# Expert rows through DRAM tables by slot, stationary router weights and tiles at multiples of 512 bytes in a two-layer decoder kernel

## The chip, the cores and the metric

The kernel runs on one core of one Trainium2 chip. The metric is the device time of one execution in microseconds (us), here 1588.71 us as the median of 3 runs (1586.83 to 1590.33). One execution was recorded by the hardware profiler. The engines are named as in the profile: PE is TensorE's matrix multiplier (PEld its weight loads), DVE is VectorE, ACT is ScalarE, POOL is GpSimd and SP is SyncE. SP and POOL issue DMA transfers.

## The reference

The trunk has two layers over 256 tokens of width 1024, in float32. Each layer does a mixer (a combined projection, sparse attention and a pooling branch, merged and projected back) and then a channel mixer. In layer 0 the channel mixer is a dense SwiGLU, in layer 1 it is a mixture of 8 experts of which each token uses the best two. The change touches the second one:

```python
def moe_swiglu(h, w_router, w1, w3, w2):
    logits = jnp.einsum('bsd,de->bse', h, w_router)
    top_v, top_i = lax.top_k(logits, 2)
    top_w = jax.nn.softmax(top_v, axis=-1)
    gate = jnp.sum(one_hot(top_i, 8) * top_w[..., None], axis=-2)
    y = jnp.zeros_like(h)
    for e in range(8):
        y = y + gate[..., e:e + 1] * ((silu(h @ w1[e]) * (h @ w3[e])) @ w2[e])
    return y          # w1, w3: 8 x 1024 x 3584, w2: 8 x 3584 x 1024
```

## The kernel before

**Precision and weights.** Every large product is made of three matmuls in a reduced-precision float32 form: an operand is split into a high and a low part, and high by high, high by low and low by high are added in PSUM (`three`, lines 744 to 748). Weights come in chunks of 128 x 2048 or 128 x 1024 floats. SP loads a chunk into `w_raw`, ACT rounds it to `w_hi` (line 448 in layer 1's experts, 442 elsewhere), DVE subtracts to get `w_lo` (line 1125 or 1120), and PE multiplies. `w_hi` and `w_lo` have four slots each. The raw chunks have four slots in the layers and eight in the expert stage, where `w_raw` holds chunks with number modulo 8 below 4 and `w_raw_456` and `w_raw_7` the others. Both splits wait for PE to free a slot, so they run up to four chunks ahead of it. SP loads up to eight chunks ahead. Each engine's instructions are written out in order by hand, and semaphores join them. There is no scheduler.

**Expert jobs.** Tokens are sorted to experts in jobs of up to 128 rows. The number of jobs is read from a table and is 8 on these inputs (112 SiLU instructions of 14 blocks each). A job has 28 up chunks (w1 and w3 side by side, 14 blocks of 2 chunks, 12 matmuls of 512 columns per chunk) and 28 down chunks (6 matmuls each). After each block ACT takes the SiLU (line 695), DVE multiplies (line 1536), PE transposes the product (line 1060), and ACT and DVE split it again (lines 700 and 1542).

**Rows in and out.** DVE writes for each job a selection matrix `select` with a one where token and slot meet (`select`, line 1461). PE gathers the job's rows already transposed by 32 matmuls of 128 columns, x high and low against `select` (`gather`, line 1034), and ACT and DVE scale and split them (lines 680 and 1515). The gather of job i+1 stands between the up and the down part of job i. For the way back PE transposes `select` (line 1078), and after the down part ACT and DVE split the result y in two (lines 737 and 1577). PE scatters it to token order by 8 matmuls of 512 columns (`scatter`, line 1045). This is placed in the next job, after the first chunk of its second block. DVE then adds the rows times the gate to `x_residual` (line 1523). Job 0 scatters zeros, which POOL has written (line 423). After the last job the scatter comes once more, and SP stores the output (line 408).

**Routing.** Before the jobs PE multiplies h by the router weights with h as the stationary operand, 48 matmuls of 8 columns. DVE takes the norm's inverse root, the logits (line 1430), the two best experts and a mask. PE counts positions with five small fp32 matmuls (lines 1020 to 1024), DVE writes the low part of the token rows (line 1448), the selection for job 0 and the job table.

## Time and profile before

| | |
|---|---|
| profiled execution, device time | 1589.16 us |
| its span, first to last instruction | 1587.3 us |
| PE busy | 1547.0 us, 97% of the span |
| DVE busy | 1267.5 us, 80% |
| ACT busy | 1052.3 us, 66% |
| DMA, mean over the span | 281 GB/s, 445.32 MB |
| DMA from 40 to 200 us, in layer 0 | 129 to 186 GB/s |
| mean granted TensorE clock | 0.988 of full speed |

A busy share is an average. PE is pipelined, so a PE that is always busy can still issue at less than its best rate, and the starts of matmuls tell more than their durations. In the expert stage a matmul of 512 columns lasts 0.39 us in the records, while the next one starts 0.23 us after it. The clock is given as a share of full speed, 1.00 for 2.4 GHz and 0.50 for 1.2 GHz. A releaser in square brackets is what ended an engine's idle time.

### The profile page before, as it was taken

The numbers are of one execution on the slowest core, as the hardware profiler recorded it, in microseconds if no ns is written. First come the engines' busy times: TensorE is split into PE (matmuls) and PEld (weight loads), VectorE is DVE, ScalarE is ACT, GpSimd is POOL, SyncE is SP. The second block draws the span as 40 slices with busy tenths as digits, with TensorE's granted clock in tenths as the row PEclk, the third lists the DMA queues.
The fourth block names the chain that finished last, engine by engine and source line by source line (L and its number), as shares of the span: only waits on it lengthen the run. The fifth ranks groups of instructions, "written<-read, shape, count | busy, mean of one in ns | idle before, by whom it ended". The sixth has DMA issues, their size and how long they took to land.

```text
span 1587.3 us, 22532 instructions
## 1 busy us (share of the span) xinstructions
PE 1547.0 (97%) x7253; PEld 1270.7 (80%) x7253; DVE 1267.5 (80%) x1329; ACT 1052.3 (66%) x1159; POOL 5.9 (0%) x12
## 2 busy tenths in 40 slices
PE   7999999999999899999999999999999999999997
PEld 6888888788888778878878878877887887887885
DVE  5885655446976579799789789799889979978978
ACT  6565544336464467687687687687778768768766
POOL 0000000000000000000000000000000000000000
PEclk9999999999999789999999999999999999999998
DMA  9543565358543669799899999999989989989985
GB/s 333 160 162 129 186 202 167 106 190 283 167 160 108 234 228 305 262 367 371 290 379 370 313 362 367 330 340 371 373 299 372 373 292 367 369 296 376 372 296 195
DMA packets 329116, 445.32 MB, mean 281 GB/s; under 512 B 14144, under 2 KB 269160, under 8 KB 329080
## 3 DMA queue, kind: packets, MB, share of 16 engines
q1 hardware_dynamic: 328512, 442.71, 81.8%
q0 software_dynamic: 480, 2.13, 0.4%
q8 instruction: 20, 0.33, 0.1%
q14 instruction: 16, 0.13, 0.0%
q10 hardware_dynamic: 88, 0.02, 0.0%
HBM read 443.76 MB, written 1.05 MB: 280 GB/s over the span
## 4 chain that ended last, share of the span: by engine, by line
PE 83%; DMA 4%; issue 4%; DVE 4%; ACT 3%; SPq 1%; DVEq 0%; ACTq 0%
PE bank L746 26%; PE bank L748 25%; PE bank L747 25%; DMA w_raw<-in_moe_w 4%; PE bank L1034 2%; ACT w_hi L448 2%; PE bank L1060 2%; DVE w_lo L1125 1%; DVE hT_lo L1515 1%; SPq L351 1%; PE bank L828 1%; DMA w_raw<-in_w_in 1%; PE bank L772 1%; ACT hT_hi L737 0%; PE bank L812 0%
## 5 line engine op out<-in xcount | busy, mean ns | idle before, releaser
L1125 DVE TENSOR_TENSOR w_lo<-w_raw,w_hi 128x1024 fp32r<-128x1024 f32 (+1 forms) x448 | 780.7, 1755 | 110.8 <-ACT w_hi L448 110.2
L448 ACT ACTIVATE w_hi<-w_raw 128x1024 fp32r<-128x1024 f32 (+1 forms) x448 | 663.8, 1492 | 157.6 <-PE bank L748 143.8
L746 PE MATMUL bank<-w_hi,hT_hi 128*128 128x512 f32 (+1 forms) x1424 | 567.5, 399 | 6.6 <-DVE hT_lo L1515 2.5
L748 PE MATMUL bank<-w_hi,hT_lo 128*128 128x512 f32 (+1 forms) x1424 | 554.9, 390 | 0.0
L747 PE MATMUL bank<-w_lo,hT_hi 128*128 128x512 f32 (+1 forms) x1424 | 553.6, 389 | 0.0
L746 PEld LDWEIGHTS bank<-w_hi,hT_hi 128*128 128x128 f32 x1424 | 268.7, 189 | 62.3 <-issue 6.8
L748 PEld LDWEIGHTS bank<-w_hi,hT_lo 128*128 128x128 f32 x1424 | 268.5, 189 | 56.6
L747 PEld LDWEIGHTS bank<-w_lo,hT_hi 128*128 128x128 f32 x1424 | 269.2, 189 | 50.8
L1120 DVE TENSOR_TENSOR w_lo<-w_raw,w_hi 128x2048 fp32r<-128x2048 f32 (+2 forms) x100 | 201.5, 2019 | 95.6 <-ACT w_hi L442 94.8
L442 ACT ACTIVATE w_hi<-w_raw 128x2048 fp32r<-128x2048 f32 (+2 forms) x100 | 169.6, 1699 | 160.1 <-PE bank L748 158.6
L746 PE MATMUL bank<-w_hi,hiddenM_hi 128*128 128x512 f32 x448 | 178.7, 399 | 1.1
L748 PE MATMUL bank<-w_hi,hiddenM_lo 128*128 128x512 f32 x448 | 176.8, 395 | 0.0
L747 PE MATMUL bank<-w_lo,hiddenM_hi 128*128 128x512 f32 x448 | 176.7, 394 | 0.0
L695 ACT ACTIVATE hiddenM<-bank 128x256 f32<-128x256 f32 x112 | 42.8, 382 | 99.2 <-PE bank L748 99.2
L746 PEld LDWEIGHTS bank<-w_hi,hiddenM_hi 128*128 128x128 f32 x448 | 84.4, 188 | 23.3 <-DVE w_lo L1125 4.6
L748 PEld LDWEIGHTS bank<-w_hi,hiddenM_lo 128*128 128x128 f32 x448 | 84.4, 188 | 19.7
L747 PEld LDWEIGHTS bank<-w_lo,hiddenM_hi 128*128 128x128 f32 x448 | 84.5, 189 | 18.7
L1536 DVE TENSOR_TENSOR hiddenM<-hiddenM,bank 128x256 f32<-128x256 f32 x112 | 46.0, 410 | 7.9 <-ACT hiddenM L695 6.9
L1060 PE MATMUL bank<-shape_constants,hiddenM 128*128 128x128 f32 x224 | 43.1, 274 | 7.0 <-DVE hiddenM L1536 7.0
L1060 PEld LDWEIGHTS bank<-shape_constants,hiddenM 128*128 128x128 f32 x224 | 29.5, 139 | 25.0 <-DVE hiddenM L1536 13.8
L1542 DVE TENSOR_TENSOR hiddenM_lo<-bank,hiddenM_hi 128x256 fp32r<-128x256 f32 x112 | 46.6, 416 | 0.0
L700 ACT ACTIVATE hiddenM_hi<-bank 128x256 f32 (+1 forms) x112 | 41.2, 368 | 0.2 <-PE bank L1060 0.2
(230 smaller groups left out, 1022.9 us busy)
## 6 DMA issues: line engine op xcount, KB each, us to landing
w_raw<-in_moe_w SPq DMA_DIRECT2D x672, 512.0 KB
w_raw<-in_w_in SPq DMA_DIRECT2D x64, 512.0 KB
w_raw<-in_dense_w SPq DMA_DIRECT2D x44, 512.0 KB
w_raw<-in_dense_w SPq DMA_DIRECT2D x44, 256.0 KB
w_raw<-in_w_out SPq DMA_DIRECT2D x16, 512.0 KB
w_raw<-in_w_pool_proj SPq DMA_DIRECT2D x8, 512.0 KB
w_raw<-in_w_attn_proj SPq DMA_DIRECT2D x8, 512.0 KB
w_raw<-in_w_in SPq DMA_DIRECT2D x8, 296.0 KB
```

Of the source, the lines that this page charges most:

```text
L442: act.activation(whi[:, c % SLOTS, 0:n], raw[:, c % SLOTS, 0:n], ACT.Copy).then_inc(s_hi, 1)
L448: act.activation(whi[:, m % SLOTS, 0:n], raw8[m % 8][:, 0:n], ACT.Copy).then_inc(s_hi, 1)
L695: act.activation(hsM[:, q, :], bank[4 + q][:, 0:256], ACT.Silu).then_inc(m_si, 1)
L700: act.activation(dst, bank[q][:, 0:256].rearrange("p (k t) -> p k t", t=P), ACT.Copy).then_inc(m_fhi, 1)
L746: pe.matmul(dst, ahi, bhi, start=start, stop=False)
L747: pe.matmul(dst, ahi, blo, start=False, stop=False)
L748: return pe.matmul(dst, alo, bhi, start=False, stop=stop)
L1060: ins = pe.transpose(bank[q][:, f * P:f * P + P], hsM[:, q, f * P:f * P + P], ident)
L1120: dve.tensor_tensor(wlo[:, s, 0:n], raw[:, s, 0:n], whi[:, s, 0:n], ALU.subtract).then_inc(s_lo, 1)
L1125: dve.tensor_tensor(wlo[:, m % SLOTS, 0:n], raw8[m % 8][:, 0:n], whi[:, m % SLOTS, 0:n], ALU.subtract).then_inc(s_lo, 1)
L1536: dve.tensor_tensor(hsM[:, q, :], hsM[:, q, :], bank[4 + q][:, 256:512], ALU.mult).then_inc(m_hm, 1)
L1542: dve.tensor_tensor(lo, bank[q][:, 0:256].rearrange("p (k t) -> p k t", t=P), hi, ALU.subtract).then_inc(m_flo, 1)
```

## The change

**Rows by slot.** The kernel gets two tables in DRAM, `x_by_slot` and `y_by_slot`, with 12 x 128 rows of 1024 floats. During layer 0 SP copies parts of x into all of the first and a part of the second, 16 transfers of 512 KB. After routing, ACT scales the token rows once more into `x_scaled_rows`, and POOL writes them to their slots by four indirect transfers of 512 KB (128 rows of 4 KB), one for each half of the tokens and each of their two choices. Each later job loads its 128 rows with one SP transfer, and PE only transposes them (8 fp32 transposes). Job 0 is still gathered by `select`. After a job's down part ACT copies y to SBUF in fp32, and SP stores it to `y_by_slot`. The scatter, its selection transposes, y's low part and DVE's additions in the loop are gone. After the last job POOL gathers each token's two rows by four indirect transfers, and DVE adds them with their gates.

**Router.** The router weights are now the stationary operand: 24 matmuls with 8 output rows and 256 columns. PE transposes the 8 x 256 result back. DVE's norm moves behind the copy of that result. ACT loads its square root table earlier. DVE writes the low part of the second half of the rows after the selection instead of before. `keep_busy` adds 22 matmuls of 512 columns, whose results nobody reads, at four places.

**Addresses.** The small tensors are allocated first, with a pad of 48 words, so that the large ones start at multiples of 512 bytes. Before, in each partition, `w_raw` started at 128 modulo 512 bytes, and `w_raw_7` and `w_raw_456` at 256 modulo 512.

```diff
+        sq0 = sb("sqrt_first", [P, 16])
+        sb("align_512", [P, 48])
+        raw = sb("w_raw", [P, SLOTS, FULL])
+        whi = sb("w_hi", [P, SLOTS, FULL], FR)
+        wlo = sb("w_lo", [P, SLOTS, FULL], FR)
+        X = sb("x_residual", [P, TT, D])
+        hThi = sb("hT_hi", [P, KC, S], FR)
+        hTlo = sb("hT_lo", [P, KC, S], FR)
         ident = cst[:, C_ID:C_ID + P]
 
...
         moe.close()
+        late = ExitStack()
+        sb("late_raws", [P, 4, FULL], F32, late)
+        xg = sb("x_slot_rows", [P, D], F32, late)
+        ysb = sb("y_slot_rows", [P, D], F32, late)
+        y0 = sb("y_first_choice", [P, TT, D], F32, late)
+        sb("late_hidden", [P, D], F32, late)
+        xn = sb("x_scaled_rows", [P, TT, D], F32, late)
+        yg = [[y[:, t, :] for t in range(TT)] for y in (y0, xn)]
+        late.close()
+        xslot = nc.dram_tensor("x_by_slot", (NJ * P, D), F32).ap()
+        yslot = nc.dram_tensor("y_by_slot", (NJ * P, D), F32).ap()
...
-                for col in ZCOL:
+                fill = [xslot[P * j:P * j + P, :] for j in range(NJ)] + [yslot[P * j:P * j + P, :] for j in range(E, NJ)]
+                for q, col in enumerate(ZCOL):
                     for h in range(2):
                         load(c, k_halves(c, w, 512 * h, col, 512))
+                        if l == 0:
+                            if c == 2:
+                                sp.wait_ge(s_x, 16)
+                            sp.dma_start(fill[2 * q + h], X[:, h, :]).then_inc(s_xz, 16)
                         c += 1
...
                 group(up_chunk, i, e, 24, 6)
+                sp.wait_ge(s_xsc, 2 * TT * 16)
+                sp.wait_ge(s_g, i * 2 + 2)
+                sp.dma_start(xg[:], xslot[bass.ds(i * P + P, P), :]).then_inc(s_xg, 16)
                 group(down_chunk, i, e, 28, 0)
                 with sp.Fori(0, 3) as it:
                     for u in range(2):
                         group(down_chunk, i, e, 32 + 4 * u, it * 2 + (1 + u), it * 8)
 
+            def store_y(i):
+
+                sp.wait_ge(m_y, i * 2 + (LEAD + 2))
+                sp.dma_start(yslot[bass.ds(i * P, P), :], ysb[:]).then_inc(s_ys, 16)
+
             def next_job(i, e):
 
                 for g in range(2):
                     group(up_chunk, i, e, JOB_CHUNKS + 4 * g, g)
+                store_y(i)
...
+            store_y(njobs - 1)
+            sp.wait_ge(s_ys, njobs * 16 + 16)
+            sp.nop().then_inc(s_go, 1)
             for t in range(TT):
-                sp.wait_ge(m_xa, njobs * 4 + (2 * t + 2))
+                sp.wait_ge(m_xa, 2 * t + 2)
                 sp.dma_start(out[0, t * P:t * P + P, :], X[:, t, :]).then_inc(s_out, 16)
...
-            pool.wait_ge(s_rt, 1)
-            for z in (yhi, ylo, selT[:]):
-                ins = pool.memset(z.bitcast(F32), 0.0)
-            ins.then_inc(s_y0, 1)
+            pool.wait_ge(s_xz, (2 * NJ - E) * 16)
+            pool.wait_ge(s_row, 1)
+            for c in range(2):
+                for t in range(TT):
+                    if c == 0:
+                        pool.wait_ge(s_xn, t + 1)
+                    pool.indirect_dma_start(xslot, bass.IndirectOffsetOnAxis(rowu[:, c * TT + t:c * TT + t + 1], 0),
+                                            xn[:, t, :], None).then_inc(s_xsc, 16)
+            pool.wait_ge(s_go, 1)
+            for t in range(TT):
+                for c in range(2):
+                    pool.indirect_dma_start(yg[c][t], None, yslot,
+                                            bass.IndirectOffsetOnAxis(rowu[:, c * TT + t:c * TT + t + 1], 0)
+                                            ).then_inc(s_yg[c * TT + t], 16)
...
+                else:
+                    act.activation(sq0[:, 0:1], cst[:, C_ONE:C_ONE + 1], ACT.Sqrt)
...
             gathered_hi(0)
+            for t in range(TT):
+                act.activation(xn[:, t, :], X[:, t, :], ACT.Copy, scale=st[:, 3, t:t + 1]).then_inc(s_xn, 1)
+            act.nop().then_inc(m_y, LEAD)
+            act.nop().then_inc(s_ys, 16)
...
@@ -709,8 +757,7 @@
                         if not (first and u == 0):
                             hid_hi_m(b - 1, 1 - u)
                         if first and u == 1:
-                            act.wait_ge(s_st, i + 1)
-                            act.activation(selT[:], bank[1][:, 0:S], ACT.Copy).then_inc(s_sts, 1)
+                            act.wait_ge(s_xsc, 2 * TT * 16)
                         silu_m(b, u)
...
                 act.wait_ge(s_use, i * JOB_CHUNKS + (MOE0 + JOB_CHUNKS))
+                act.wait_ge(s_ys, i * 16 + 16)
                 for j in range(2):
-                    act.activation(yhi[:, 4 * j:4 * j + 4, :], bank[6 + j][:].rearrange("p (k n) -> p k n", n=P),
-                                   ACT.Copy).then_inc(m_yhi, 1)
+                    act.activation(ysb[:, 512 * j:512 * j + 512], bank[6 + j][:], ACT.Copy).then_inc(m_y, 1)
                 split_m(d0 + 27, FULL, j8)
...
+            def keep_busy(n, b):
+
+                for _ in range(n):
+                    pe.matmul(bank[b][:], aThi[:, 0, 0:P], aThi[:, 0:2, :], start=True, stop=True)
+
             layer(1, LAYER1, first=lambda: x_T(2, 1))
+            keep_busy(4, 5)
             x_T(3, 1)
...
                 for k in (2 * j, 2 * j + 1):
-                    for t in range(TT):
-                        ins = three(bank[4 + t][:, 0:E], hThi[:, k, t * P:t * P + P], hTlo[:, k, t * P:t * P + P],
-                                    wrhi[:, k, :], wrlo[:, k, :], k == 0, k == KC - 1)
+                    ins = three(bank[4][0:E, 0:S], wrhi[:, k, :], wrlo[:, k, :], hThi[:, k, :], hTlo[:, k, :],
+                                k == 0, k == KC - 1)
             ins.then_inc(s_rt, 1)
+            pe.wait_ge(s_lt, 1)
+            for t in range(TT):
+                ins = pe.transpose(bank[5][:, t * E:t * E + E], lgT[:, t * P:t * P + P], cst[0:E, C_ID:C_ID + E])
+            ins.then_inc(s_rl, 1)
+            keep_busy(9, 0)
...
+            keep_busy(3, 0)
 
             def gather(i):
 
-                pe.wait_ge(s_sel, i + 1)
+                if isinstance(i, int):
+                    pe.wait_ge(s_sel, 1)
+                    for t in range(TT):
+                        pe.wait_ge(s_xrl, t + 1)
+                        for j in range(2):
+                            for q in range(4):
+                                k = 4 * j + q
+                                for x in (xrhi, xrlo):
+                                    ins = pe.matmul(bank[2 + j][:, q * P:q * P + P], x[:, t, k * P:k * P + P],
+                                                    selR[:, t, :], start=(t == 0 and q == 0 and x is xrhi),
+                                                    stop=(t == TT - 1 and x is xrlo), skip_group_check=True)
+                            if t == TT - 1:
+                                ins.then_inc(s_g, 1)
+                    return
+                pe.wait_ge(s_xg, i * 16)
                 for j in range(2):
                     for q in range(4):
                         k = 4 * j + q
-                        for t in range(TT):
-                            for x in (xrhi, xrlo):
-                                ins = pe.matmul(bank[2 + j][:, q * P:q * P + P], x[:, t, k * P:k * P + P],
-                                                selR[:, t, :], start=(t == 0 and x is xrhi),
-                                                stop=(t == TT - 1 and x is xrlo))
+                        ins = pe.transpose(bank[2 + j][:, q * P:q * P + P], xg[:, k * P:k * P + P], ident)
                     ins.then_inc(s_g, 1)
...
-            pe.wait_ge(s_xrl, 2)
             gather(0)
-            pe.wait_ge(s_y0, 1)
+            keep_busy(6, 0)
             pe.wait_ge(s_tab, 1)
...
                         chunk(c, [bank[4 + u][:]], hehi, helo, 0, 512, True, False, i * jd + it, tiles=1)
-                        if first and u == 1:
-                            scatter(i)
                         if not (first and u == 0):
                             if not first:
                                 pe.wait_ge(m_flo, i * NB_E + b - 2 + LEAD)
                             hiddenT_m(b - 1, 1 - u)
-                        if first and u == 1:
-                            for t in range(TT):
-                                ins = pe.matmul(bank[1][:, t * P:t * P + P], selR[:, t, :], identR[:],
-                                                start=True, stop=True)
-                            ins.then_inc(s_st, 1)
...
-                pe.wait_ge(m_xa, i * 4 + 4)
                 gather(i + 1)
...
-                        pe.wait_ge(m_xa, i * 4 + 4)
+                        pe.wait_ge(m_y, i * 2 + LEAD)
...
-            scatter(njobs)
...
             dve.wait_ge(s_rt, 1)
+            dve.tensor_copy(lgT, bank[4][0:E, 0:S]).then_inc(s_lt, 1)
+            norm(3)
+            dve.wait_ge(s_rl, 1)
             for t in range(TT):
-                ins = dve.tensor_scalar(lg[:, t, :], bank[4 + t][:, 0:E], st[:, 3, t:t + 1], None, ALU.mult)
+                ins = dve.tensor_scalar(lg[:, t, :], bank[5][:, t * E:t * E + E], st[:, 3, t:t + 1], None, ALU.mult)
...
+            rows_lo(0)
             dve.wait_ge(s_pos, 1)
...
+            for t in range(TT):
+                ins = dve.tensor_scalar(selR[:, t, :], cst[:, C_IOTA:C_IOTA + P], pm[:, t, 0:1], None, ALU.is_equal)
+            ins.then_inc(s_sel, 1)
+            rows_lo(1)
...
+            iotas = cst[:, C_IOTA:C_IOTA + E].rearrange("p (o e) -> p o e", o=1)
+            dve.tensor_tensor(picke[:], pick[:], iotas.broadcast_to([P, nq, E]), ALU.mult)
+            dve.tensor_scalar(past[:], pm[:], float(P), None, ALU.is_ge)
+            dve.scalar_tensor_tensor(rowe[:], iotas.broadcast_to([P, TT, E]), float(P), pm[:], ALU.mult, ALU.add)
+            chain(dve.scalar_tensor_tensor(one8, iota8, -1.0, rank, ALU.mult, ALU.add))
+            dve.tensor_reduce(tabf[:, E:NJ], picke[:], AX.X, ALU.add)
+            chain(dve.tensor_scalar(one8, one8, float(E - 2), float(P), ALU.add, ALU.mult))
+            chain(dve.tensor_tensor(past[:], past[:], ov[:, 3:4, :].broadcast_to([P, TT, E]), ALU.mult))
             dve.tensor_copy(tabi[:], tabf[:]).then_inc(s_tab, 1)
-            chain(dve.tensor_scalar(posj[:, :, E:NJ].rearrange("p t q -> p q t"), pickr[:], -float(P), None, ALU.add))
+            chain(dve.tensor_tensor(rowe[:], rowe[:], past[:], ALU.add))
+            for c, m in enumerate((m0, m1)):
+                ins = dve.tensor_tensor(rowc[:, c], m[:], rowe[:], ALU.mult)
+            chain(ins)
+            chain(dve.tensor_reduce(rowf[:], rowc[:].rearrange("p c t e -> p (c t) e"), AX.X, ALU.add))
+            dve.tensor_copy(rowu[:], rowf[:]).then_inc(s_row, 1)
 
...
-                        if 1 <= b <= 4:
-                            add_rows(i, (b - 1) // 2, (b - 1) % 2)
-                        if b == 5:
-                            dve.wait_ge(s_st, i + 1)
-                            select(i + 1)
...
-                for j in range(2):
-                    dve.wait_ge(m_yhi, i * 2 + j + 1)
-                    dve.tensor_tensor(ylo[:, 4 * j:4 * j + 4, :], bank[6 + j][:].rearrange("p (k n) -> p k n", n=P),
-                                      yhi[:, 4 * j:4 * j + 4, :], ALU.subtract).then_inc(m_ylo, 1)
                 split_m(d0 + 27, FULL, j8)
             for t in range(TT):
-                for nh in range(2):
-                    add_rows(njobs, t, nh)
+                for c in range(2):
+                    dve.wait_ge(s_yg[c * TT + t], 16)
+                    if c:
+                        dve.wait_ge(m_xa, 2 * t + 1)
+                    dve.scalar_tensor_tensor(X[:, t, :], yg[c][t], pr[:, 2 + c, t:t + 1], X[:, t, :],
+                                             ALU.mult, ALU.add).then_inc(m_xa, 1)
...
```

On PE, in the second block of each job, before: `select` is the selection matrix, `hT_hi` and `hT_lo` in line 1045 hold y's parts, and `hiddenM` is the block's product.

```order
L748 MATMUL bank<-w_hi,hT_lo 128x512
L1045 MATMUL bank<-hT_hi,selectT 128x512
L1045 MATMUL bank<-hT_lo,selectT 128x512
...
L1058 REGISTER_ALU
L1060 MATMUL bank<-shape_constants,hiddenM 128x128 x2
L1078 MATMUL bank<-identity_r,select 128x128 x2
L756 REGISTER_ALU
L746 MATMUL bank<-w_hi,hT_hi 128x512
```

And at the same place now:

```order
L795 MATMUL bank<-w_hi,hT_lo 128x512
L1115 REGISTER_ALU
L1117 MATMUL bank<-shape_constants,hiddenM 128x128 x2
L803 REGISTER_ALU
L793 MATMUL bank<-w_hi,hT_hi 128x512
```

The eight scatter matmuls and the two of the selection are gone, so the transposes of the product follow the first chunk directly. At the gather of the next job PE now has, where 32 matmuls of line 1034 stood:

```order
L1135 COMPARE_AND_BRANCH
L1100 ISA
L1104 MATMUL bank<-shape_constants,x_slot_rows 128x128 x8
L1143 REGISTER_ALU
L1147 ISA
L793 MATMUL bank<-w_hi,hiddenM_hi 128x512
```

Only the 8 transposes of the loaded rows are left between up and down part. On SP the load of these rows stands between the last up chunk and the first down chunk of a job, and in another place the store of y behind the second group of the next job's up chunks:

```order
L372 DMA w_raw<-in_moe_w 128x4x256 x2
L393 ISA
L394 ISA
L394 DMA x_slot_rows<-x_by_slot 128x1024
L383 REGISTER_ALU
L377 ISA
L377 DMA w_raw<-in_moe_w 128x1024
...
L402 REGISTER_ALU
L403 ISA
L403 DMA y_by_slot<-y_slot_rows 128x1024
```

Both wait on SP for a semaphore (the gather before, and y in SBUF), and the chunk loads behind them wait with them.

## Rows read from the trace of the kernel before

**Rows 1.** The page's chain that ended last: shares of the span by engine.
```profile
PE 83%; DMA 4%; issue 4%; DVE 4%; ACT 3%; SPq 1%; DVEq 0%; ACTq 0%
```

**Rows 2.** Windows from gather to gather: length, each engine's busy us, clock, DMA share, GB/s.
```profile
770.88:897.12 126.24, 125.39 (x576) 102.06 (x575) 112.29 (x100) 95.04 (x97) 0.00 (x0) 1.00 1.01 349
...
sum 886.34, PE 877.26 PEld 714.46 DVE 786.51 ACT 665.37 POOL 0.00; mean PE 125.32 PEld 102.07 DVE 112.36 ACT 95.05 POOL 0.00
```

**Rows 3.** Timeline of TensorE, one steady gather: start, duration, engine, line, operation.
```profile
770.88 0.23 PE L1034 MATMUL bank<-select,x_rows_hi 128*128 128x128 f32 x1
...
774.41 0.45 PE L746 MATMUL bank<-w_hi,hiddenM_hi 128*128 128x512 f32 x1
```

**Rows 4.** Timeline of TensorE in layer 1: eight fp32 transposes between matmuls.
```profile
529.13 0.39 PE L748 MATMUL bank<-w_hi,hT_lo 128*128 128x512 f32 x1
529.36 1.04 PE L772 MATMUL bank<-shape_constants,x_residual 128*128 128x128 f32 x8
...
530.47 0.39 PE L747 MATMUL bank<-w_lo,hT_hi 128*128 128x512 f32 x1
```

**Rows 5.** Timeline of all engines, end of one expert job and start of the next.
```profile
814.45 1.92 ACT L448 ACTIVATE w_hi<-w_raw 128x2048 fp32r<-128x2048 f32 x1 [0.56 <-DMA w_raw<-in_moe_w]
...
822.77 0.40 PE L1045 MATMUL bank<-hT_hi,selectT 128*128 128x512 f32 x1
...
824.88 0.41 DVE L1536 TENSOR_TENSOR hiddenM<-hiddenM,bank 128x256 f32<-128x256 f32 x1
...
825.35 0.44 PE L1060 MATMUL bank<-shape_constants,hiddenM 128*128 128x128 f32 x2 [0.55 <-DVE hiddenM L1536]
```

**Rows 6.** DMA throughput in 40 slices of 3.25 us, from 700 to 830 us.
```profile
GB/s 381 350 348 354 385 385 385 382 348 349 355 384 386 385 381 348 349 367 422 418 387 266 171 161 134 271 260 284 338 413 417 413 368 348 349 352 385 386 385 379
```

**Rows 7.** Waits over the span: engine, line, what for, total us, times, longest.
```profile
ACT w_hi L448 <- DMA w_raw<-in_moe_w: 13.6, 17, 1.1
```

**Rows 8.** Timeline of TensorE, first job, where the empty scatter stands.
```profile
570.51 0.41 PE L1045 MATMUL bank<-hT_hi,selectT 128*128 128x512 f32 x1
...
572.37 0.38 PE L1060 MATMUL bank<-shape_constants,hiddenM 128*128 128x128 f32 x2
```

**Rows 9.** Windows in the routing stage and at the first job's start.
```profile
537.50:550.00 12.50, 8.62 (x41) 8.44 (x40) 6.95 (x28) 7.02 (x10) 2.12 (x3) 0.50 1.08 377
...
560.00:565.00 5.00, 5.00 (x12) 3.98 (x13) 3.68 (x12) 1.66 (x3) 0.00 (x0) 0.52 0.29 97
```

**Rows 10.** Timeline of the routing stage, all engines.
```profile
538.87 1.28 ACT L474 ACT_TABLE_LOAD   x1
...
541.20 0.16 DVE L1151 TENSOR_TENSOR norm_stats<-norm_stats 128x2 f32<-128x2 f32 x1
...
543.86 0.36 DVE L1430 TENSOR_SCALAR router_logits<-bank,norm_stats 128x8 f32<-128x8 f32 x2 [2.51 <-PE bank L748]
...
546.78 2.48 DVE L1448 SCALAR_TENSOR_TENSOR x_rows_lo<-x_residual,norm_stats,x_rows_hi 128x1024 fp32r<-128x1024 f32 x2
...
557.07 0.41 PE L1034 MATMUL bank<-select,x_rows_lo 128*128 128x128 f32 x1
...
559.97 0.79 PE L746 MATMUL bank<-w_hi,hT_hi 128*128 128x512 f32 x1 [2.48 <-DVE hT_lo L1515]
```

**Rows 11.** Timeline of the end of the kernel.
```profile
1574.99 1.06 ACT L737 ACTIVATE hT_hi<-bank 128x512 fp32r<-128x512 f32 x2
...
1581.53 2.71 DVE L1523 SCALAR_TENSOR_TENSOR x_residual<-bank,gate_by_job,x_residual 128x512 f32<-128x512 f32 x4
...
1582.95 1.65 SPq L408 DMA_DIRECT2D out<-x_residual  x2
```

**Rows 12.** DMA issues: queue, count, KB each, median us from issue to landing.
```profile
x_residual<-in_x SPq DMA_DIRECT2D x1, 1024.0 KB, 6.7
out<-x_residual SPq DMA_DIRECT2D x2, 512.0 KB, 2.7
...
w_router<-in_moe_router POOLq DMA_DIRECT2D x1, 32.0 KB, 8.4
```

86 lines of the change are left out of this document (23 added, 63 removed).

## The prediction

> **What bounds the kernel now.** I read the chain that ended last first. PE is 83% of it and DMA 4% [rows 1], so what counts is how fast PE issues. Next came windows cut from one gather to the next, since the expert jobs are most of the span. Seven of them take 886.34 us, 126.62 us a job, all at full clock, with PE busy 125.3 us, DVE 112.4 us and ACT 95.0 us of it, and DMA at 349 GB/s [rows 2]. PE paces the job and the DMA is close behind. What one removed instruction is worth is therefore read from starts on PE's timeline, and only where PE doesn't then wait for something else [rows 3 to 5]. Then the DMA's rate inside a job [rows 6, 7], the routing stage [rows 9, 10] and the end [rows 11, 12].
>
> **Gathers.** From the first of 32 matmuls to the next matmul it is 774.41 - 770.88 = 3.53 us [rows 3]. Eight fp32 transposes between matmuls of 512 columns stretch 529.13 to 530.47 us. Less two matmul starts of 0.23 us, that is 0.88 us [rows 4]. The gathers for jobs 1 to 8 each save 2.65 us (the last one's rows go unused, but it runs): 21.2 us. The load of the slot rows is queued before the first down chunk, some twelve chunks ahead of PE, and is hidden by them. If it were late, PE would stop for up to 2.7 us, a 512 KB transfer [rows 12].
>
> **Scatter and selection transposes.** The eight scatter matmuls start at 822.77 us and the block's transposes at 825.35 us, with 0.55 us of idle PE in between. PE waits there for DVE's product, which ends at 824.88 + 0.41 = 825.29 us [rows 5]. This product stays where it is when the scatter goes, because it ends a chain on ACT and DVE: a split, the copies of y, a split, the SiLU table, a split, SiLU, a split, the product. So the 1.86 us of the scatter turn into waiting. The chain begins with 0.56 us of waiting for DMA at 814.45 us [rows 5]. I count those 0.56 us as won at seven job starts, 3.9 us, because the DMA gets faster (below). The bounds are 0, and 7 x 1.1 us, the longest such wait [rows 7]: 7.7 us. In job 0 nothing is waited for, and the scatter's 572.37 - 570.51 = 1.86 us go in full [rows 8]. Two selection matmuls at 3.53/32 = 0.11 us each, in eight jobs: 1.8 us. DVE loses its additions (4 x 0.68 us from [rows 11]) and y's low part. It had room, so this is worth nothing by itself.
>
> **Routing.** Before, the logits start at 543.86 us because the router's matmuls end late. The norm ends at 541.20 + 0.16 us, and 1.28 us of that chain was a table load [rows 10]. Now 24 matmuls replace 48, and the norm ends the path, 1.28 us earlier for the table and about 0.6 us later for the copy of the 8 x 256 logits that it follows: 540.8 us, 3.1 us won. The selection follows one row split of 2.48/2 = 1.24 us instead of two, and one small copy fewer: 1.4 us. The gather takes 557.07 - 550.42 + 0.21 = 6.86 us, because the clock was granted at 0.50 here [rows 9, 10]. With the added matmuls in the pauses I take it at full clock, 3.5 us: 3.3 us won. DVE's longer table of rows now stands ahead of the low parts that PE waits for: about 0.7 us lost. Together the first job starts 7.1 us earlier than 559.97 us. Its first 12 matmuls took 5.0 us at clock 0.52 [rows 9]. At 0.23 us each it is 2.8 us: 2.2 us won. The 22 added matmuls (5 us in all) lie in pauses of 1.4 to 2.9 us. If the clock stays at 1.2 GHz they fill them exactly.
>
> **Start.** SP now waits for x, which lands 6.7 us after its issue [rows 12], and puts a 512 KB transfer before chunk 3. At 385 GB/s [rows 6] that is 1.36 us on a chunk that PE needs several us later. I take 0.5 us between 0 and 1.4. The 16 fills are 22 us of DMA time spread beside layer 0's first block products, where the queue moves less than half of what rows 6 show possible. POOL's four writes to the slots start at about 552 us, and at 2.7 us each end at 563 us. ACT waits for them before the second block's SiLU at about 564 us, so they are just covered.
>
> **End.** y is copied at 1574.99 + 1.06 = 1576.05 us, and the kernel ends at 1587.3 us [rows 11]. Now follow the store (0.3 us to issue, 2.7 us), four indirect gathers, one addition of 1.24 us and the output transfer of 2.8 us. No row shows an indirect transfer. The four lie between 2.7 + 3 x 1.36 = 6.8 us (overlapping at 385 GB/s) and 4 x 8.4 us, the POOL transfer at the crowded start [rows 12]. I take 4 x 2.7 = 10.8 us, by the row for transfers of this size. The end is then 1593.9 us: 6.6 us lost, between 2.6 and 29.4. The Trainium skill (DMA: Bandwidth & Descriptors, "Anatomy of one DMA — SWDGE (gpsimd) path") gives about 2 us plus bytes at 436 GB/s for a transfer from POOL. By that one is 3.2 us, four in a row 12.8 us, and the end 2 us later. No row shows it.
>
> **Addresses.** Within the up part the DMA runs at 381 to 386 GB/s in some slices and 348 to 355 in others, in turns of about four [rows 6]. Four chunks take about as long as such a turn, and the slow turn is the last one before the down chunks, which start in `w_raw_456`: the slow slots are those of `w_raw`, at 128 modulo 512 bytes, the fast ones lie at 256. So I take all up chunks at 385 GB/s. A job's DMA is then 29.4 MB/385 + 14.7 MB/418 + 1.05 MB/385 = 76.3 + 35.1 + 2.7 = 114 us (before: 80 + 35), under PE's new 126.62 - 2.65 - 0.22 - 0.56 = 123.2 us. Store and load of rows then fit. The Trainium skill (same page, "How a descriptor splits into AXI transactions") says that a run that doesn't start at 256 bytes pays for an extra partial transaction; the trace agrees as far as 348 against 385 can.
>
> **Sum.** Won: 21.2 + 3.9 + 1.9 + 1.8 + 7.1 + 2.2 = 38.1 us. Lost: 6.6 + 0.5 = 7.1 us. Net 31.0 us from the profiled execution's 1589.16 us (span 1587.3 us): 1558.2 us. That execution was 0.4 us above the median, so 1558 us.
>
> **Rivals.** *The clock falls in routing all the same* (18%). The large pause for the mask remains, nearly 2 us after the nine fillers. Then the gather's 3.3 us and the 2.2 us aren't won: 1563 or 1564 us. *The waits for DMA stay*, because addresses aren't the reason for the two rates (8%): the 3.9 us go, 1562 us. *The DMA paces the jobs* (4%): this is the slower side. If 349 GB/s [rows 2] is all it can give over a job, 44.04 + 1.05 MB take 129.2 us, 2.6 us more than now. The seven jobs lose 18 us instead of gaining 24, and with the rest the time is about 1601 us. It decides once a job's DMA passes 123.2 us, at 366 GB/s. Against it stand 385 and 418 GB/s for tens of us, and slices of 134 to 171 in the down part where nothing is left to load [rows 6]. *A ceiling just above* (3%): the Trainium skill (same page, "Where 436 GB/s comes from") has the HBM side bind at about 358 GB/s. As a mechanism it is the same one. The 45.09 MB would take 126.0 us, the loop would stay as it is, and only routing and end would change: 1580 us. The slices above 380 speak against it. *POOL's indirect transfers are slow* (4%), 8.4 us each in a row: the slots are written at 586 us, PE stops some 20 us, and the end costs 29.4 us: 1602 us. Even with 6.9 us each they would eat the whole gain. *It doesn't do what it says* (1%): row slots beside the path, no change.
>
> **How the numbers follow.** My case has 62%: 1558 us. With its own bounds (job starts 0 to 7.7, end 2.6 upwards, start 0 to 1.4) it spans 1551 to 1564. The clock and DMA-wait rivals end inside 1564. Up to 1567 for both together, the range 1550 to 1567 leaves out the 12% of the other cases and a few per cent of mine. A measurement of this kernel can tell about 0.2%, 3 us, from no change. Slower by more: 4 + 4%, less a little where a slow POOL is only half as slow: 6%. Same: 2%. Faster: 92%.
>
> **What would show it.** Right: steady jobs of 123.2 us from gather to gather; the transposes in 0.9 us; at the second block a PE wait of about 2 us for DVE's product where the scatter was; no ACT waits for `w_raw` there; up slices all near 385 GB/s; the first expert matmul near 553 us into the span at clock 1.00; 18 us from y's copy to the end. Wrong: jobs above 125 us, a DMA share at its top all through the down part, PE waiting for the slot rows or ACT for the slot writes, or an end of over 25 us.

## The result and the profile after

The changed kernel takes 1560.33 us (median of 4 runs, 1559.3 to 1560.9), the kernel before 1589.32 us on the same chip: a ratio of 0.9818, 95% interval 0.9803 to 0.9832. The forecast was 1558 us, between 1550 and 1567. The profiled execution has a span of 1558.9 us against 1587.3 us before, so 28.4 us are to be accounted for, where the sum of the prediction had 31.0.

Cut at the same four places as before, the span reads like this (us, from TensorE's timeline):

| stretch | before | after | won | forecast |
|---|---|---|---|---|
| start to the first expert matmul | 559.97 | 554.16 | 5.8 | 6.6 |
| from there to the first steady gather (job 0) | 83.97 | 82.07 | 1.9 | 4.3 |
| seven jobs, gather to gather | 886.34 | 861.96 | 24.4 | 24.0 |
| last gather to the end | 57.02 | 60.71 | -3.7 | -3.9 |

The windows from gather to gather, after: length, then busy us of TensorE, its weight loads, VectorE, ScalarE and GpSimd, the granted clock, DMA's share and GB/s. They answer to [rows 2].
```profile
636.23:760.35 124.12, 121.26 (x542) 98.80 (x541) 109.05 (x92) 94.65 (x96) 0.00 (x0) 0.99 1.02 364
760.35:882.63 122.28, 119.90 (x541) 97.54 (x540) 108.80 (x92) 94.67 (x96) 0.00 (x0) 1.00 1.02 370
882.63:1007.07 124.44, 121.28 (x542) 98.76 (x541) 109.17 (x92) 94.79 (x96) 0.00 (x0) 0.99 1.01 362
...
sum 861.96, PE 842.02 PEld 685.28 DVE 762.58 ACT 662.86 POOL 0.00; mean PE 120.29 PEld 97.90 DVE 108.94 ACT 94.69 POOL 0.00
```
A job takes 123.14 us instead of 126.62, as forecast (123.2). But TensorE is busy for 120.3 us of it, where before it was busy for 125.3 of 126.6: there are now 2.8 us of waiting in a job instead of 1.3. And two of the seven jobs are about 1.6 us longer than the rest, with a clock below 1.00.

TensorE at one steady gather, after (answers to [rows 3]): start, duration, what.
```profile
882.39 0.40 PE L795 MATMUL bank<-w_hi,hT_lo 128*128 128x512 f32 x1
882.63 1.03 PE L1104 MATMUL bank<-shape_constants,x_slot_rows 128*128 128x128 f32 x8
883.42 0.48 PE L793 MATMUL bank<-w_hi,hiddenM_hi 128*128 128x512 f32 x1
```
It is 883.42 - 882.63 = 0.79 us to the next matmul, where it was 3.53. No wait stands ahead of it: the slot rows are there.

TensorE in the down part, 18 matmul starts apart, first before, then after:
```profile
789.74 0.39 PE L746 MATMUL bank<-w_hi,hiddenM_hi 128*128 128x512 f32 x1
...
793.93 0.39 PE L746 MATMUL bank<-w_hi,hiddenM_hi 128*128 128x512 f32 x1
```
```profile
889.89 0.40 PE L793 MATMUL bank<-w_hi,hiddenM_hi 128*128 128x512 f32 x1
...
893.99 0.39 PE L793 MATMUL bank<-w_hi,hiddenM_hi 128*128 128x512 f32 x1
```
The starts are (793.93 - 789.74)/18 = 0.233 us apart before and (893.99 - 889.89)/18 = 0.228 after; over all jobs the means are 0.2327 and 0.2272. The whole down part takes 38.78 us instead of 39.50.

ScalarE, VectorE and TensorE at the end of one job and the start of the next, after (answers to [rows 5]); a bracket is the idle time just before and what ended it.
```profile
804.70 1.28 ACT L739 ACT_TABLE_LOAD   x1
...
806.11 1.90 ACT L491 ACTIVATE w_hi<-w_raw 128x2048 fp32r<-128x2048 f32 x1
...
808.04 2.29 DVE L1173 TENSOR_TENSOR w_lo<-w_raw,w_hi 128x2048 fp32r<-128x2048 f32 x1 [0.94 <-ACT w_hi L491]
...
810.25 0.41 DVE L1573 TENSOR_TENSOR hiddenM<-hiddenM,bank 128x256 f32<-128x256 f32 x1
...
810.72 0.44 PE L1117 MATMUL bank<-shape_constants,hiddenM 128*128 128x128 f32 x2 [1.71 <-DVE hiddenM L1573]
```
Where the scatter stood, TensorE waits 1.71 us for VectorE's product (1.7 to 2.65 us in the seven jobs), as forecast. From the last down matmul to these transposes it is 11.32 us as the mean of the seven jobs, where it was 11.88: 0.56 us less, also as forecast.

DMA throughput from 700 to 830 us, 3.25 us a slice (answers to [rows 6]), and the waits for it over the span.
```profile
GB/s 387 384 386 385 384 387 384 386 385 385 386 384 386 401 420 421 357 281 199 199 260 333 197 324 369 396 416 412 381 384 385 385 385 386 401 382 386 385 385 386
```
```profile
ACT w_hi L491 <- DMA w_raw<-in_moe_w: 21.2, 28, 1.5
...
ACT hiddenM L743 <- DMA x_by_slot<-x_scaled_rows,row_of_choice: 3.3, 1, 3.3
```
All slices of the up part are at 385 now; those at 348 are gone. Yet ScalarE waits longer for weights in all (21.2 us against 13.6 in [rows 7]). A new wait of 3.3 us, in job 0, is for GpSimd's writes to the slots.

The end, after (answers to [rows 11]).
```profile
1539.52 1.06 ACT L785 ACTIVATE y_slot_rows<-bank 128x512 f32<-128x512 f32 x2
...
1540.76 0.35 SPq L403 DMA_DIRECT2D y_by_slot<-y_slot_rows  x1
1543.71 2.09 POOL L465 DMA_INDIRECT y_first_choice<-y_by_slot,row_of_choice  x1 [980.79 <-SPq L438]
...
1549.13 1.28 DVE L1613 SCALAR_TENSOR_TENSOR x_residual<-y_first_choice,gate_probs,x_residual 128x1024 f32<-128x1024 f32 x1 [4.19 <-DMA y_first_choice<-y_by_slot,row_of_choice]
...
1552.61 3.69 SPq L441 DMA_DIRECT2D out<-x_residual  x2
...
1554.65 1.28 DVE L1613 SCALAR_TENSOR_TENSOR x_residual<-x_scaled_rows,gate_probs,x_residual 128x1024 f32<-128x1024 f32 x1
```
From y's copy (ends 1540.58) to the end at 1558.9 it is 18.3 us (forecast: 18). The store takes 2.95 us, the first indirect read 5.4 us to its addition, and the four overlap.

One more view, the page's chain that ended last, now reads "issue 63%; PE 33%" instead of "PE 83%" [rows 1], though TensorE is busy for 97% of the span before and 96% after. It is no measure of what changed.

### The profile page after: what moved, and what is told of

It reads as the page before. It is cut to its first block, busy times and chain, and to the rows that moved or that the text cites. A ratio compares the mean times of both kernels' runs of the same rounds, so it can differ in the third digit from the quotient of the medians.

```text
span 1558.9 us, 21888 instructions
## 1 busy us (share of the span) xinstructions
PE 1501.7 (96%) x6973; PEld 1230.8 (79%) x6973; DVE 1241.6 (80%) x1264; ACT 1051.4 (67%) x1153; POOL 16.1 (1%) x17
## 4 chain that ended last, share of the span: by engine, by line
issue 63%; PE 33%; DVE 1%; DMA 1%; POOL 1%; ACT 0%; POOLq 0%; SPq 0%; ACTq 0%; DVEq 0%
PE bank L793 10%; PE bank L795 10%; PE bank L794 10%; PE bank L875 1%; DMA w_raw<-in_w_in 1%; PE bank L819 1%; POOL x_by_slot L460 0%; PE bank L1094 0%; PE bank L859 0%; DMA y_first_choice<-y_by_slot,row_of_choice 0%; PE bank L930 0%; PE bank L1007 0%; PE bank L910 0%; PE bank L847 0%; PE bank L938 0%
```

## The experiments

Each ran in three rounds beside the kernel before. Times are medians of 4 runs; those of the kernel before in the same sessions were 1589.3 to 1590.0 us. Where three numbers stand in brackets, they are the ratio to the kernel before and its 95% interval. "The job" is the mean of the seven windows of one profiled execution.

Small differences need care. (6), (7), (8) and (10) come out 1.6 to 3.5 us below the changed kernel, and the interval of each overlaps the changed kernel's (0.9803 to 0.9832). What they show is therefore read stage by stage in the profiled executions. How much these vary by themselves can be seen in (5), (7), (9), (10) and (11), whose edits lie outside TensorE's work in the seven jobs: 859.95 to 862.88 us for the seven.

| kernel | time, us | job, us | down part, us |
|---|---|---|---|
| before | 1589.3 | 126.62 | 39.50 |
| before, all at 512 (1) | 1577.3 | 125.15 | 38.79 |
| changed, addresses of before (2) | 1579.3 | 125.01 | 39.55 |
| changed, w_raw at 128 (3) | 1572.7 | 124.88 | 38.78 |
| changed, all off (4) | 1598.4 | 128.20 | 39.05 |
| changed | 1560.3 | 123.14 | 38.78 |
| changed, four more edits (12) | 1548.9 | 121.71 | 38.78 |

**1. The addresses alone, in the kernel before.**
```
+        sb("align_512", [P, 64])
         raw = sb("w_raw", [P, SLOTS, FULL])     # and the other large tiles, behind the small ones
```


> The kernel before with one change: the small tensors stand first and a pad follows, so that every large tile starts at a multiple of 512 bytes. Theory: the addresses alone make two things that the trace after shows: the up part's loads all run at about 385 GB/s (before in turns 348 and 385), and the down part, whose matmuls started 0.2327 us apart, gets 0.2272 us and 38.8 us a job instead of 39.5. With about 0.5 us less waiting at each job's start that is 8 x 0.72 + 7 x 0.5 = 9 us: about 1580 us, seven jobs of 125.4 us instead of 126.6. Rival: the down part got faster because DVE's additions and y's low part are gone; then only the DMA's slices change, the down part stays at 39.5 us, and the time is 1585 to 1589 us.


Measured: 1577.34 us (0.993, 0.9913 to 0.9948). The down part takes 38.79 us, with all the DVE work still in it, and the boundary is 0.76 us shorter (11.12 us from the last down matmul to the second block's transposes, against 11.88). The windows:
```profile
768.46:893.51 125.05, 124.47 (x575) 102.06 (x574) 112.19 (x100) 94.95 (x97) 0.00 (x0) 1.00 0.99 353
...
sum 876.06, PE 871.16 PEld 714.22 DVE 785.75 ACT 664.73 POOL 0.00; mean PE 124.45 PEld 102.03 DVE 112.25 ACT 94.96 POOL 0.00
```
The theory holds, and it gave more than expected: 10.3 us in the seven jobs. The addresses are a gain of their own, on TensorE as well. The up part's slices are all at about 385 GB/s.

**2. The changed kernel at the addresses of before** (w_raw, w_hi, w_lo at 128 modulo 512 bytes, w_raw_7 and w_raw_456 at 256).
```
-        sb("align_512", [P, 48])                # large tiles first again
+        sb("sqrt_pad", [P, 112])
```


> The changed kernel with all large tiles at the addresses that they have in the kernel before (w_raw, w_hi and w_lo at 128 modulo 512 bytes, w_raw_7 and w_raw_456 at 256). It is the change without its last part. Theory: the DMA binds the jobs. Half of the up chunks load at 348 GB/s, as in the run with w_raw alone at 128, where a job took 124.9 us; the down part, at 39.5 us instead of 38.8, gives the DMA back some of its time. So jobs of 125 to 126 us and about 1575 us: the rows through DRAM without the addresses are worth 15 us, the addresses 15 us here. Rival (TensorE still binds and each part adds its own): jobs of 123.1 + 0.7 + 0.5 us, 1570 us.


Measured: 1579.33 us, of runs of 1573.9 (the profiled one), 1579.3, 1579.35 and 1579.6. DMA throughput from 830 to 960 us:
```profile
GB/s 385 386 385 358 348 348 375 385 385 385 358 348 350 404 420 421 421 340 160 224 335 258 300 377 412 412 394 364 349 348 371 386 384 402 374 348 348 358 385 386
```
The turns are back, and the job is 125.01 us. That is the theory's number and not the rival's 124.3, but the time is 4 us above the theory's 1575. The profiled execution is 5.4 us shorter than its three siblings, which have no trace; part of it may be the routing stage, which ran at full clock all through (below, 9). So the rows through DRAM alone are worth 10.4 us, the addresses alone 12.6 us (1), and both together 29 us. That both give 6 us more than the sum I put down to the DMA, which has more to carry once the rows go through DRAM; (3) makes it likely and no run splits it off.

**3. Only w_raw off**, w_hi, w_lo and the rest at multiples of 512.
```
-        sb("align_512", [P, 48])
+        sb("align_512", [P, 48 + 32])           # and 96 words behind w_raw
```


> The changed kernel with w_raw alone moved to 128 modulo 512 bytes; w_hi, w_lo and all others stay at multiples of 512. It tells the DMA's part from TensorE's part. If the DMA's rate hangs on where it writes and the spacing of the down matmuls on where TensorE reads: slices of 348 GB/s come back, the down part stays at 38.8 us, the job starts lose 0.5 us or so each: 1563 to 1565 us. If both hang on w_raw (the slow writes disturb TensorE's reads): the down part is 39.5 us too, 1570 us.


Measured: 1572.70 us (0.9894, 0.9878 to 0.9911), job 124.88 us, down part 38.78 us, the slices again in turns of 385 and 348 to 349. The two effects separate as the first theory said: the DMA's rate goes with where it writes, and the spacing of the down matmuls doesn't go with `w_raw`, so it must go with another tile. But the price was mis-sized: I had 3 to 5 us, it is 12.4. A job is 1.74 us longer, and 1.0 of it lies between the last down matmul and the second block's transposes (12.32 us instead of 11.32), the rest behind them. So it is a delay at the job's start after all, two and a half to four times what I took. It isn't a bound on the whole job: in the down part the DMA still catches up, with slices down to 185 GB/s.

**4. All large tiles off** (w_raw, w_hi, w_lo at 128, w_raw_7 and w_raw_456 at 320).
```
-        sb("align_512", [P, 48])                # large tiles first, no pad
```


> The changed kernel with the old order of the tensors (w_raw at 128 modulo 512 bytes, the others off as before). Theory: the down part goes back to 39.5 us a job, the slow DMA turns of 348 GB/s come back, and the waits at the job starts grow by about 0.5 us or more, since a job now carries 45.1 MB: about 9 to 12 us more than the changed kernel, 1570 to 1572 us. Rival (addresses do nothing but for the DMA): 1560 to 1564 us with the down part at 38.8 us.


Measured: 1598.39 us (1.0056, 1.004 to 1.0073): slower than the kernel before. I had thought that these were the old addresses; the new tensor of 64 bytes moved the other slots from 256 to 320, so that no slot loads fast. A window, the waits and ScalarE's splits in the up part:
```profile
766.31:894.63 128.32, 122.24 (x542) 96.79 (x541) 109.07 (x92) 95.92 (x96) 0.00 (x0) 1.00 1.05 351
```
```profile
ACT w_hi L490 <- DMA w_raw<-in_moe_w: 137.0, 172, 2.3
```
```profile
838.73 1.93 ACT L490 ACTIVATE w_hi<-w_raw 128x2048 fp32r<-128x2048 f32 x1 [1.09 <-DMA w_raw<-in_moe_w]
...
841.75 1.93 ACT L490 ACTIVATE w_hi<-w_raw 128x2048 fp32r<-128x2048 f32 x1 [0.46 <-DMA w_raw<-in_moe_w]
844.76 1.93 ACT L490 ACTIVATE w_hi<-w_raw 128x2048 fp32r<-128x2048 f32 x1 [1.08 <-DMA w_raw<-in_moe_w]
```
A chunk each 3.01 us is 1.049 MB at 348 GB/s; TensorE needs one each 2.853 us, which is 367 GB/s. So 348 is too slow for it, 385 (2.72 us a chunk) is enough, and half of each, 2.87 us on average, lies at the edge. This is my slower rival (the DMA paces the jobs: 129.2 us a job, 1601 us), met nearly to the number. The down part is 39.05 us here and 39.55 in (2), with starts 0.2290 and 0.2325 us apart, though w_hi and w_lo, its moving tiles, lie at 128 in both. What differs for TensorE is `hiddenM_hi` and `hiddenM_lo`, its stationary tiles: at 256 modulo 512 in the kernel before and in (2), at 320 here, at 0 in the changed kernel, (1) and (3). And the up part reads the same w_hi and w_lo at 0.228 us a start in all six kernels. So `hiddenM` is the first suspect; no run moved it alone.

**5. The added matmuls out.**
```
-            keep_busy(4, 5)                     # and (9, 0), (3, 0), (6, 0)
```


> The changed kernel without the 22 added matmuls that read aT_hi in the routing stage. Theory: they put off the fall of the clock from the router's matmuls (before) to the middle of the gather, and the six behind the gather bring it back early. Without them the clock falls to its half some 5 us earlier, the positions and the whole gather run at half rate, and the first 12 expert matmuls take 5 us instead of 2.7: 2.5 to 3.5 us more than the changed kernel, 1563 to 1564 us. Rival: they bought nothing beyond the pauses they fill, since the gather ran at half rate all the same: within 1 us of 1560.3.


Measured: 1560.23 us, the same. The rival was right about the time. The profile, of the slowest of the four executions (1562.84 us), shows that the added matmuls do act: the low clock lasts from 543.5 to 560.5 us instead of 545.1 to 555.4, and the first 12 expert matmuls take 5.1 us, as in the kernel before, instead of 3.4. But job 0 takes 82.06 us, no more than the changed kernel's 82.07, since two waits that TensorE has there in the changed kernel (0.71 and 0.62 us, see 7) are absent. The first expert matmul comes 1.5 us later, 555.68 us, and 1.0 of that is there when the router starts.

**6. A filler where the scatter was.**
```
+                        if first and u == 1:
+                            for _ in range(8):
+                                pe.matmul(bank[2][:], hehi[:, 0, :], hehi[:, 0:4, :], start=True, stop=True)
```


> The changed kernel with eight matmuls of 512 columns (their result is used by nothing) where the scatter's eight stood, ahead of the second block's transposes of each job. Theory: TensorE waits 1.7 to 2.65 us there for DVE's product, and in two of seven jobs the granted clock falls behind that wait and costs 1.2 us. The matmuls (1.86 us) fill the wait without moving its end; the clock stays at 1.00 in all jobs, and the seven jobs take 2 to 2.5 us less: about 1558 us. Rival (the matmuls delay what follows, or the fall has another cause): 0 to 3 us more than the changed kernel, jobs of 124 us with a clock of 0.99 stay.


Measured: 1556.83 us. The seven jobs take 857.31 us, 4.7 less than the changed kernel's. TensorE before the second block:
```profile
807.59 1.98 PE L1129 MATMUL bank<-hT_hi 128*128 128x512 f32 x8
809.65 0.44 PE L1117 MATMUL bank<-shape_constants,hiddenM 128*128 128x128 f32 x2
```
No wait of note is left here (0 to 0.1 us in six jobs, 0.8 in the first), and no job has a clock below 1.00 (eight matmuls in a stretch that was idle cost nothing). In the changed kernel the fall is seen around the wait of 2.35 us at 687 us, one window with it and the next:
```profile
684.00:690.00 6.00, 3.65 (x15) 2.70 (x14) 5.41 (x4) 4.82 (x5) 0.00 (x0) 0.88 1.08 394
690.00:700.00 10.00, 10.00 (x42) 8.12 (x42) 7.66 (x7) 6.57 (x6) 0.00 (x0) 0.90 1.08 384
```
From the second block to the next gather such jobs take 73.1 us, the others 71.9, and with the fillers all take 71.7 to 72.0: that is 2.5 of the 4.7 us. The other 2.1 lie ahead of the transposes (11.03 us instead of 11.32); (11), which has no fillers, has 11.03 there too, so they are chance as far as can be told. It isn't the wait's length alone that decides: one of 2.38 us in the same execution brought no fall.

**7. The scaled rows earlier.**
```
+            for t in range(TT):                 # moved ahead of gathered_hi(0)
+                act.activation(xn[:, t, :], X[:, t, :], ACT.Copy, scale=st[:, 3, t:t + 1]).then_inc(s_xn, 1)
             gathered_hi(0)
```


> The changed kernel with ACT's two copies of the scaled rows ahead of the first gather's column copies, in the 5.7 us that ACT waits there, instead of behind them. Theory: POOL's writes to the slots then start when the rows are known, at about 549 us instead of 554.8, and land some 5 us earlier; ACT's wait of 3.3 us ahead of the second block's SiLU in job 0, and TensorE's waits of 0.7 and 0.6 us behind it, go: the first job (554.16 to 636.23 us) takes 1.3 to 2 us less, 1558.5 us. Rival: POOL's issue and the transfers' length decide, and the wait only shrinks to 1 us or so with nothing won at TensorE.


Measured: 1557.25 us; job 0 takes 80.48 us instead of 82.07. GpSimd starts its writes at 550.13 us instead of 554.79, and the wait for them is gone from the list. The prediction had ended the four writes at 563 us; ScalarE got past its wait at 568.72. But (10) and (11), whose job 0 is that of the changed kernel, took 80.8 us for it without this edit. GpSimd's fourth write, in the changed kernel and in (11):
```profile
559.98 2.94 POOL L460 DMA_INDIRECT x_by_slot<-x_scaled_rows,row_of_choice  x1 [0.30 <-issue]
```
```profile
559.97 0.95 POOL L464 DMA_INDIRECT x_by_slot<-x_scaled_rows,row_of_choice  x1 [0.30 <-issue]
```
Where it takes 0.95 us, ScalarE waits 1.5 or 1.8 us instead of 3.3 and TensorE not at all. So the edit removes ScalarE's wait, but most of the 1.6 us comes also without it, when this one instruction is short. What makes it long is open.

**8. The SiLU table loaded once.**
```
-                act.activation(silu0[:], cst[:, C_ONE:C_ONE + 1], ACT.Silu)     # head of the loop
+            act.activation(silu0[:], cst[:, C_ONE:C_ONE + 1], ACT.Silu)         # ahead of the loop
```


> The changed kernel with the one-column SiLU that loads ACT's table moved from the head of the job's loop to ahead of the loop, so that the table is loaded once and not in every job (1.28 + 0.2 us of ACT each). Theory: since the scatter is gone, TensorE waits at each second block for a chain of ACT and DVE work of which this load is a link; without it the wait of 1.7 to 2.65 us shrinks by 1.3 to 1.5 us in each of seven jobs, and the clock doesn't fall there: 7 x 1.4 + 2.4 = 12 us less, about 1548 us. Rival: another link (DVE's splits, or DMA's late chunk) ends last once the load is gone: 0.5 us a job, about 1556 us.


Measured: 1557.72 us: far from the theory's 1548, near the rival's 1556. The seven jobs take 859.99 us, at the lower edge of what unchanged jobs show. From the last down matmul to the second block's transposes it is 10.6 us instead of 11.3, but from there to the next gather 72.4 to 73.3 us instead of 71.9. The waits:
```profile
ACT w_hi L491 <- DMA w_raw<-in_moe_w: 39.7, 47, 2.7
```
They were 21.2 us, 28 times. Work that comes earlier meets chunks that do not. No job has a low clock here, so the longer stretch is not the clock.

**9. The router's matmuls as before.**
```
-                    ins = three(bank[4][0:E, 0:S], wrhi[:, k, :], wrlo[:, k, :], hThi[:, k, :], hTlo[:, k, :],
+                    for t in range(TT):
+                        ins = three(bank[4 + t][:, 0:E], hThi[:, k, t * P:t * P + P], ...
```


> The changed kernel with the router's 48 matmuls of 8 columns as before (the rows stationary, no copy and transposes of the logits); the preloaded square-root table and the added matmuls stay. Theory: the 3.1 us that the logits come earlier were the table load and the clock, not the orientation. With the table preloaded the norm ends near 540.2 us, and at full clock 48 matmuls end near 541 us (535.2 + 48 x 0.113 us), so the first expert matmul comes 0 to 1 us later than in the changed kernel, and the time is 1560 to 1561.5 us. Rival: a stretch of matmuls of 8 columns brings the clock down, as it did in the kernel before at 537.5 us; then they end at 543.5 us, the gather runs at half rate, and the first expert matmul comes 2.5 to 3.5 us later: 1563 us.


Measured: 1564.28 us, 4 us more; first expert matmul at 558.94 us, 4.8 us later. TensorE, and the windows of the changed kernel and of (2) in the gather:
```profile
537.59 0.25 PE L795 MATMUL bank<-w_router_hi,hT_lo 128*128 128x8 f32 x1
537.70 0.30 PE L793 MATMUL bank<-w_router_hi,hT_hi 128*128 128x8 f32 x1
537.86 0.36 PE L794 MATMUL bank<-w_router_lo,hT_hi 128*128 128x8 f32 x1
538.08 0.35 PE L795 MATMUL bank<-w_router_hi,hT_lo 128*128 128x8 f32 x1
```
```profile
544.50:552.00 7.50, 7.40 (x35) 7.08 (x34) 4.87 (x29) 1.43 (x6) 0.00 (x0) 0.54 1.09 383
```
```profile
544.50:552.00 7.50, 6.63 (x47) 5.57 (x46) 7.04 (x36) 4.08 (x10) 0.00 (x0) 1.00 1.09 379
```
The rival was right. With 8 columns the starts go from 0.11 to 0.21 us apart at 537.7 us, in an unbroken row of matmuls. With the weights stationary the clock holds until 545.1 us, in the first matmuls of the gather. In (2), which has the same instructions there, it held all the way. From the start of the gather to the first expert matmul that took 6.4 us instead of 9.3, and the first 12 expert matmuls 2.8 us. So the stationary weights gain through the clock. That the gather runs at full clock was seen in one of the 11 profiled executions with stationary weights, none of them a second one of the same kernel; whether it is chance or comes from (2)'s addresses was not tried.

**10. Four plain reads at the end instead of indirect ones.**
```
-                    pool.indirect_dma_start(yg[c][t], None, yslot, ...
+                    pool.dma_start(yg[c][t], yslot[P * (2 * t + c):P * (2 * t + c) + P, :]
```


> The changed kernel with the last four transfers as plain reads of fixed rows of the table instead of indirect reads by row number (so what they read isn't what the reference adds). It gives the price of the indirection. If it costs little: each lands some 5.5 us after its issue as now, within 1 us of 1560.3. If the indirection is dear (a descriptor for each of 128 rows of 4 KB made on POOL): the end becomes 2 to 5 us shorter, 1555 to 1558 us.


Measured: 1558.72 us (it reads fixed rows, so its output isn't the reference's), and in the profile 18.5 us from the last matmul to the end instead of 21.2. GpSimd spends 0.55 us on a plain issue, 0.94 to 2.1 us on an indirect one; the first addition comes 3.5 us after the first issue instead of 5.4. In these two executions the indirection costs 2.7 us of the end; the medians differ by 1.6.

**11. One more read of 512 KB in each job.**
```
+                sp.dma_start(y0[:, 0, :], xslot[bass.ds(i * P + P, P), :]).then_inc(s_more, 16)
```


> The changed kernel with one more read of 512 KB from the table in each job, right behind the load of the slot rows, into a place that is used by nothing until the end. It asks how much room the DMA has. Theory: a loop that takes 122 to 123 us is at the DMA's limit around the job's start, where ACT waits for chunks 28 times; the read costs 1.36 us of DMA at 385 GB/s, and most of it appears in each job: jobs of 124 us, 7 to 9 us more, 1568 us. Rival (114 us of transfers per job leave room, the read falls into the idle DMA of the down part): 0 to 2 us more.


Measured: 1560.54 us, jobs of 122.98 us: nothing. The theory fell. Behind the last up chunk, where the down part's chunks need less than the DMA gives, a transfer is free. What binds around the job's start is not the job's sum of bytes, but what stands in the queue at that place.

**12. Four edits together**: (7), (8), (6) with four matmuls, and the store of y later in SP's queue.
```
                 group(up_chunk, i, e, 24, 6)
+                if last_y:
+                    store_y(i, -1)              # was behind the next job's first eight chunks
```


> The changed kernel with four edits: the SiLU table loaded once ahead of the loop; ACT's scaled rows ahead of the first gather's column copies; four matmuls of 512 columns (used by nothing) in TensorE's wait at each second block, for the clock; and the store of a job's y moved in SP's queue from behind the next job's first eight chunks to behind its last up chunk, where the DMA has caught up. Theory: the table's 1.5 us a job were given back because the DMA was late behind the store; with the store moved the waits behind the second block go, and the gains add up: 7 x 1.3 + 1.6 + 2.4 = 13 us, 1547 us, jobs of 121.3 us. Rival (the DMA's total per job binds, wherever the store stands): jobs of 122.3 us, 1553 us.


Measured: 1548.92 us (0.9744, 0.9727 to 0.976), jobs of 121.71 us. The longest single wait for weights is 0.8 us instead of 1.5 (8: 2.7), and from the second block to the next gather it is 71.6 us instead of 71.9 or 72.6. It beats both kernels, by 41 us (of its own session) and 11. The store's move was not run by itself, and this kernel has the other three edits too, so none of the 11 us is given to one of them.

## Why the prediction came out right, point by point

The time was right within 0.2%, and so was the largest term. But of its parts several were wrong in both directions and partly cancelled. The clearest case is the seven jobs, 24.4 us won against 24.0. By parts it is 19.1 us for the gathers (forecast 18.6) and 3.9 up to the second block's transposes (3.9), as said; but 5.1 in the down part (forecast nothing), and a loss of 3.7 behind the second block where 1.5 were to be won. That these two cancel is luck.

**Right, with the mechanism.** The gathers: 2.65 us each forecast, 3.53 - 0.79 = 2.74 measured, 21.9 us for eight. The scatter's time became waiting for VectorE's product (shown by (6), which fills it at no cost). The 0.56 us a job came as well, but not as described: the sign "no ACT waits for `w_raw` there" failed, with waits of 0.8 us at 810.9 us and 1.4 at 817.6. The slot rows are hidden; (11) shows that even a second load is. The end lost 60.71 - 57.02 + 2.74 + 0.72 = 7.2 us against 6.6: four reads in place of one, but they overlap.

**Addresses: half of it was missed.** The prediction read two DMA rates in [rows 6] and gave them to the slots' addresses. (1) to (4) show that this was so: a slot that starts at 0 or 256 loads at 385 GB/s, at 128 or 320 at 348. The Trainium skill (DMA: Bandwidth & Descriptors, "How a descriptor splits into AXI transactions") has a rule for the beats of 32 bytes that a run takes. By it, as an estimate, a run of 1 KB that starts 128 bytes off takes 36 instead of 32, which from 385 gives 342 GB/s. Measured were 348. At 320 the same estimate is 34 beats and 362 GB/s, and 348 were measured there too, so it tells the direction and not the size. But I priced it at the 0.56 us waits, 3.9 us in all. With the new transfers all addresses together are worth 19 us (2 against the changed kernel); `w_raw`'s alone, which is the DMA's part, 12.4 (3). What I had not seen at all is on TensorE: down matmuls start 0.2327 us apart at the addresses of before and 0.2272 with all large tiles at multiples of 512, 0.72 us a job, 5.8 us for eight. No step of the prediction had it, though the slower start was in the trace: the up part's was 0.228 on average, before and after.

**Second block to the next gather: forecast 0.22 us shorter, 0.54 longer.** 71.71 us became 72.25. One cause is the clock's fall behind the wait, 1.2 us in two of seven jobs, which (6) removed. A wait that replaces work was priced as neutral; it isn't, where it ends at a lower clock. The other, 0.2 us a job, is probably the DMA: y's store stands ahead of the chunks that the first blocks need (waits of 1.4 and 0.8 us at 817.6 and 823.0 us, where the kernel before has one of 0.7), and with it moved (12) the 71.6 us are below those of before. That the move alone did it was not shown.

**Routing: 7.1 us forecast (6.6 with the start), 5.8 measured.** The step that failed is "at full clock, 3.5 us": the gather took 551.48 - 544.84 = 6.6 us, nearly as before (6.9). My rival for the clock came true for the gather and in part for the first 12 expert matmuls, which take 3.4 us (5.1 before, 2.8 forecast). Where the clock did hold, in (2), both forecasts were met (3.5 and 2.8 us). The 22 added matmuls, which I had named as the reason, shorten the first 12 expert matmuls and do nothing to the time (5). The gather began 5.6 us earlier, where the terms ahead of it had 4.5, less 0.5 for the start. The logits came 3.4 us earlier (3.1 forecast) and the gather 2.1 us sooner behind them (1.4). (9) shows that the orientation brings most of this, because the clock doesn't fall in the router. The 0.5 us of the start isn't seen: the router begins at 535.17 us, at 535.37 before.

**Job 0: 4.3 forecast, 1.9 measured.** "So they are just covered" was wrong. GpSimd began its writes at 554.79 us, not 552, since ScalarE's copies stand behind the gather's, and the wait of 3.3 us on ScalarE made two of TensorE (0.71 and 0.62 us). "ACT for the slot writes" was one of my signs of being wrong, and it was met here. With these waits absent job 0 takes 80.5 to 80.8 us, (7), (10) and (11), so up to 1.6 us of the miss is theirs. The first 12 matmuls won 1.7 us instead of 2.2.

**The slower side.** It had 4% for "the DMA paces the jobs". (4) shows the mechanism real and the condition 19 GB/s away on one side and 18 on the other: 348, 367, 385. A shift of the other slots (and of all tiles behind them) by 64 bytes decides the sign of this change: 1579.3 us in (2), 1598.4 in (4), 1589.3 before.
